# Decoder step on one core: last four experts' token rows normed apart, results written by indirect stores

## The reference

```python
def hier_moe(x, w_rg, b_rg, w_re, b_re, w_e1, w_e3, w_e2):
    ...
    for g in range(N_GROUPS):
        a = jnp.einsum('nd,edf->nef', xf, w_e1[g])
        b = jnp.einsum('nd,edf->nef', xf, w_e3[g])
        hid = jax.nn.silu(a) * b * gates[:, g, :, None]
        y = y + jnp.einsum('nef,efd->nd', hid, w_e2[g])
...
    x = x + hier_moe(rmsnorm(x, g_ffn), w_rg, b_rg, w_re, b_re, w_e1, w_e3, w_e2)
...
    y_prompt = rmsnorm(xp, g_final)
    y_sample = rmsnorm(xs, g_final)
```

## Time and profile before

| what | us |
|---|---|
| median of 3 runs (lowest, highest) | 1066.56 (1065.76, 1069.48) |
| the profiled execution's own time | 1065.81 |
| its span | 1064.0 |
| PE, DVE, ACT, POOL busy | 999.0, 638.3, 541.6, 197.6 |

### The profile page before, as it was taken

The page is one execution under the profiler, slowest core; times in us unless marked ns, Lnnn a source line. Parts: engine busy times, 40 slices in busy tenths (PEclk is TensorE's granted clock), DMA queues, the critical chain, the costliest instruction groups (busy, mean ns, idle before and its releaser), DMA issues. The chain is left out here.

```text
span 1064.0 us, 14237 instructions
## 1 busy us (share of the span) xinstructions
PE 999.0 (94%) x5327; PEld 848.1 (80%) x5327; DVE 638.3 (60%) x1175; ACT 541.6 (51%) x918; POOL 197.6 (19%) x136
## 2 busy tenths in 40 slices
PE   8999999999999999999999999948999999999970
PEld 6998999798887689999655878847888888888850
DVE  4526756345654650002664125677999999999935
ACT  6644333305221532213545012255999999999944
POOL 0003211100000021200000300011333375642220
PEclk9999999999999999999999999967999999999995
DMA  9701111244000653103563005487999999999738
GB/s 314 217 1 59 57 42 40 99 139 173 1 1 0 225 177 113 40 20 127 232 256 139 1 37 201 159 310 300 396 392 391 384 364 390 382 387 393 284 55 335
DMA packets 55211, 203.06 MB, mean 191 GB/s; under 512 B 10710, under 2 KB 19423, under 8 KB 41575
## 3 DMA queue, kind: packets, MB, share of 16 engines
q1 hardware_dynamic: 44327, 181.61, 44.9%
q0 software_dynamic: 10816, 20.54, 7.6%
HBM read 185.06 MB, written 32.83 MB: 205 GB/s over the span
## 5 line engine op out<-in xcount | busy, mean ns | idle before, releaser
L527 PE MATMUL bank<-regA_r,regW_r 128*128 128x352 f32 (+1 forms) x456 | 148.8, 326 | 0.0
L526 PE MATMUL bank<-regA_r,regW_r 128*128 128x352 f32 (+1 forms) x456 | 148.7, 326 | 0.0
L359 POOL TENSOR_TENSOR regW_r<-regW,regW_r 128x1024 fp32r<-128x1024 f32 x19 | 47.1, 2477 | 348.7 <-ACT regW_r L346 348.6
L1525 ACT ACTIVATE regY_r<-expert_w 128x1024 fp32r<-128x1024 f32 x105 | 108.9, 1062 | 1.0 <-PE bank L527 0.9
L525 PE MATMUL bank<-expert_w_r,regS_r 128*128 128x512 f32 x256 | 103.4, 404 | 0.0
L1525 ACT ACTIVATE regW_r<-expert_w 128x1024 fp32r<-128x1024 f32 x87 | 90.2, 1061 | 6.7 <-PE bank L527 6.7
L2292 DVE TENSOR_TENSOR expert_w_r<-expert_w,regY_r 128x1024 fp32r<-128x1024 f32 x74 | 89.0, 1218 | 0.0
L525 PE MATMUL bank<-regY_r,regW_r 128*128 128x352 f32 (+1 forms) x264 | 87.3, 331 | 0.5 <-ACT regB L1206 0.5
L526 PEld LDWEIGHTS bank<-regA_r,regW_r 128*128 128x128 f32 x456 | 85.9, 188 | 0.4
L527 PEld LDWEIGHTS bank<-regA_r,regW_r 128*128 128x128 f32 x456 | 85.6, 188 | 0.0
L2466 POOL DMA_INDIRECT regW<-normed_tokens,idx x32 | 44.0, 1374 | 200.0 <-DVE idx L2201 119.6
(11 more groups left out here) (363 smaller groups left out, 2408.1 us busy)
## 6 DMA issues: line engine op xcount, KB each, us to landing
expert_w<-in_we SPq DMA_DIRECT2D x96, 1024.0 KB, 13.3
regY<-in_cache_mem_v SPq DMA_DIRECT2D x6, 1024.0 KB, 7.2
regW<-in_wbc SPq DMA_DIRECT2D x11, 512.0 KB, 3.6
regS<-in_x_prompt SPq DMA_DIRECT2D x8, 512.0 KB, 6.5
regX<-in_x_prompt SPq DMA_DIRECT2D x8, 512.0 KB, 6.6
regW<-in_wq SPq DMA_DIRECT2D x8, 512.0 KB, 3.6
regA<-in_kct SPq DMA_DIRECT2D x4, 1024.0 KB, 7.9
token_sums<-regX SPq DMA_DIRECT2D x8, 512.0 KB, 2.9
```

The costliest lines, as they stand in the source:

```text
L359: eng.tensor_tensor(lo, raw, hi.bitcast(F32), ALU.subtract).then_inc(w_lo[name], 1)
L526: nc.tensor.matmul(out, stays[1], moves[0], start=False, stop=False)
L527: ins = nc.tensor.matmul(out, stays[0], moves[0], start=False, stop=last)
L1525: nc.scalar.activation(part_hi[u % HI], part_raw[n % RAW], ACT.Copy).then_inc(m_wh, 1)
```

## The change

`LATE = 4` experts (28 to 31 in the order of the loop) no longer add their rows to `token_sums`.

- When the accumulating DMA of expert 27 has landed, SP loads all nine tiles of `token_sums` (the sample tile first) into freed parts of the weight ring (`XF`), and POOL gathers the rows of the last four experts' tokens from it (`late_sums`, into `XR`). The rows hold all that the experts 0 to 27 gave.
- The tiles are squared, normed, scaled and stored as before (`square`, `roots`, `inverse`, `scaled`, `final_store`), but while the last experts run. The sample tile and the first two prompt tiles are scaled in the turn of expert 30 on DVE, and their reciprocal roots are worked out by POOL in 14 small steps (`first_roots`); tile 2 is scaled in turn 31; the others after it.
- The rows of a late expert are added to `XR` on chip: for experts 28 to 30 by POOL (`rows_added`), for expert 31 by DVE straight from PSUM (`last_rows`). ACT squares them, DVE scales them into `YR`, and POOL writes them over the results by plain indirect DMAs (`results_out`): one to `y_sample` and one to `y_prompt` for each late expert, eight in all, those to the prompt only after all prompt tiles' stores have landed. An index out of range for the output writes nothing. Since a token's two experts lie in one group and the four late ones in four groups, no token is in two of them.
- The tail of waits on `o_go` and `s_moe` is gone where there is no spill; with a spill, all is added up and normed once more.

```diff
+        gfin = spot(0)
+        XF = [spot(1 + t) for t in range(NT)]
+        XR = [spot(1 + NT + k) for k in range(LATE)]
+        YR = [spot(1 + NT + LATE + k) for k in range(LATE)]
+        UNITS = [("tile", t) for t in (NPT, *range(NPT))] + [("rows", k) for k in range(LATE)]
+        ROOTS = [(0, 3), (3, 2), (5, 2), (7, 2), (NT, LATE - 1), (NT + LATE - 1, 1)]
...
 # SP
+            for n in range(NT):
+                weights_landed(sp, n)
+            spot_dead(sp, 0)
             load(gfin, i_["gfin"], s_cst)
+            for q in range(2):
+                sp.wait_ge(m_sc[q], 16 * len(range(q, NE - LATE, 2)))
...
+            for _, t in UNITS[:NT]:
+                sums_load(t)
+            for u, (_, t) in enumerate(UNITS[:NT]):
+                sp.wait_ge(s_fo, u + 1)
+                final_store(t)
...
 # ACT
+                if e == NE - 2:
+                    square(0)
+                    square(1)
+                if e == NE - 1:
+                    nc.scalar.activation(small[:, 2:3], small[:, 0:1], ACT.Sqrt)
                 if e >= 1:
                     y_left(e - 1)
...
                 hidden_left(e)
+                if e == NE - 2:
+                    square(2)
+                    square(3)
...
-            y_left(NE - 1)
-            act.wait_ge(o_go, 1)
+            for u, n in ROOTS[1:]:
+                for v in range(max(u, 4), u + n):
+                    square(v)
+                roots(u, n)
...
 # DVE
+                if e == NE - 1:
+                    scaled(2)
                 hidden_lo(e)
+                if e == NE - 2:
+                    dve.wait_ge(s_cst, 32)
+                    dve.wait_ge(s_rt[1], NT + 1)
+                    scaled(0)
+                    scaled(1)
...
+            for k, (u, n) in enumerate(ROOTS[1:]):
+                if k == 1:
+                    last_rows()
+                dve.wait_ge(s_frt, k + 1)
+                inverse(u, n)
+                for v in range(u, u + n):
+                    scaled(v)
...
 # POOL
+            def late_sums():
+
+                for q in range(2):
+                    g.wait_ge(m_sc[q], 16 * len(range(q, NE - LATE, 2)))
+                    g.wait_ge(m_g[q], 16 * (NE // 2))
+                for k in range(LATE):
+                    if k >= 2:
+                        rows_back(g, k - 2)
+                    spot_dead(g, 1 + NT + k)
+                    c = expert_at(NE - LATE + k)
+                    g.indirect_dma_start(out=XR[k], out_offset=None, in_=sum_dram,
...
+            def rows_added(k):
+
+                e = NE - LATE + k
+                rows_back(g, k)
+                g.wait_ge(m_yo0, e + 1)
+                g.wait_ge(m_yo1, e + 1)
+                nc.gpsimd.tensor_tensor(XR[k], XR[k], YO[e % 2], ALU.add).then_inc(s_added, 1)
...
+                if e == NE - LATE:
+                    late_sums()
+                if e > NE - LATE:
+                    rows_added(e - 1 - (NE - LATE))
+                if e == NE - 2:
+                    first_roots()
...
+            g.wait_ge(s_xh_ys, 32)
+            for k in range(LATE - 1):
+                samples_out(k)
+            g.wait_ge(s_fst, 16 * NPT)
+            for k in range(LATE):
+                prompt_out(k)
+            samples_out(LATE - 1)
```

More of the change, by code:

```diff
@@ L59 @@
 LG = 40
+LATE = 4
 NEG = -3.0e38
@@ L455, in trunk_step @@
         o_sc = sem("o_sc")
[L456 removed]
+        s_added = sem("s_added")
+        s_rows = sem("s_rows")
         s_fo = sem("s_fo")
@@ L1190, in _ @@
                                  .rearrange("a p k -> (a p) k")).then_inc(o_ix, 16)
[L1192 to L1200 removed]
+                sp.wait_ge(o_go, 2)
+                for t in range(NT):
+                    sums_load(t)
+                for t in range(NT):
+                    sp.wait_ge(s_fo, NT + t + 1)
+                    final_store(t)
+                sp.wait_ge(s_fst, 16 * 2 * NPT)
+                sp.wait_ge(s_xh_ys, 48)
         @block.scalar
@@ L1249, in _ @@
             nc.scalar.activation(small[:, 1:2], small[:, 0:1], ACT.Sqrt)
-            for h, landed in ((0, s_xh), (1, s_x[0])):
+            for h, landed in ((0, s_xh_ys), (1, s_x[0])):
                 act.wait_ge(landed, 16)
@@ L1572, in _, with square, roots @@
                     part_to_hi("down", 0, 1)
+            def square(u):
+                kind, n = UNITS[u]
+                r = rows_of(n) if kind == "tile" else P
+                if kind == "tile":
+                    sums_back(act, n)
+                elif n < LATE - 1:
+                    act.wait_ge(s_added, n + 1)
+                else:
+                    act.wait_ge(m_yo0, NE)
+                    act.wait_ge(m_yo1, NE)
+                if u > 0:
+                    act.wait_ge(s_fsq, u)
+                nc.scalar.activation(junk[0:r, :], (XF if kind == "tile" else XR)[n][0:r, :], ACT.Square,
+                                     accum_out=stat[0:r, u:u + 1]).then_inc(s_fsq, 1)
+            def roots(u, n):
+                act.wait_ge(s_fsq, u + n)
+                nc.scalar.activation(stat[:, 20 + u:20 + u + n], stat[:, u:u + n], ACT.Sqrt,
+                                     scale=1.0 / D, bias=small[:, 0:1]).then_inc(s_frt, 1)
             for e in range(NE):
@@ L2335, in _, with late_samples, inverse, scaled @@
             down_lo(0, 1)
+            def late_samples():
+                listed_at, samples_at = idx[:, expert_at(NE - LATE):NE:EPG], idx[:, NE:NE + LATE]
+                link(ts_(samples_at, listed_at, float(SEQ), float(NOWHERE), ALU.is_lt, ALU.mult))
+                link(stt(samples_at, samples_at, -float(SEQ), listed_at, ALU.add, ALU.add))
+            def inverse(u, n, r=P):
+                a, root, r0, tmp, out = (stat[0:r, c + u:c + u + n] for c in (40, 20, 60, 80, 100))
+                link(ts_(a, stat[0:r, u:u + n], 1.0 / D, EPS, ALU.mult, ALU.add))
+                inv_root(a, root, r0, tmp, out)
+            def scaled(u):
+                kind, n = UNITS[u]
+                g = stat[:, 100 + u:101 + u]
+                if kind == "tile":
+                    x = XF[n][0:rows_of(n), :]
+                    stt(x, x, g[0:rows_of(n), :], gfin[0:rows_of(n), :], ALU.mult, ALU.mult).then_inc(s_fo, 1)
+                else:
+                    spot_dead(dve, 1 + NT + LATE + n)
+                    stt(YR[n], XR[n], g, gfin, ALU.mult, ALU.mult).then_inc(s_rows, 1)
+            def last_rows():
+                rows_back(dve, LATE - 1)
+                gates = gate_of_slot[:, expert_at(NE - 1):expert_at(NE - 1) + 1]
+                for h, signal in ((0, m_yo0), (1, m_yo1)):
+                    if h == 0:
+                        dve.wait_ge(full[B_Y[0]], uses[B_Y[0]] + 1)
+                    else:
+                        used(dve, ("down", NE - 1, 1))
+                    rows = XR[LATE - 1][:, 512 * h:512 * h + 512]
+                    stt(rows, bank[B_Y[h]][:, :], gates, rows, ALU.mult, ALU.add).then_inc(signal, 1)
             for e in range(NE):
@@ L2352, in _ @@
                     place_in_table((e - 5) // 3)
+                if e == 14:
+                    late_samples()
                 if e == 16:
```

151 lines of the change are left out of this document (98 added, 53 removed).

## The result

| | before | changed |
|---|---|---|
| median of four runs, us | 1066.7 (1065.8 to 1069.5) | 1083.1 (1080.8 to 1083.8) |
| the profiled execution's time and span | 1065.8, 1064.0 | 1080.8, 1078.7 |

The ratio is 1.0141 (95% interval 1.0116 to 1.0165); the medians differ by 16.4 us, the two profiled executions by 15.0. The forecast was 1068.7 (no change), with a range from 1061 to 1075.5; it missed.

A forecast was written before the change was run, and what follows sets the result against it. PE was taken to bound the body, leaving a 32.3 us tail; 10.9 us saved there is given back by a late PE (10.1) and POOL's queue (some 11): span +2.9, time 1068.7 us, range 1061 to 1075.5.

The forecast's parts named there:

- step 4: POOL's eight indirect stores at the end: from 1052.05 to 1064.05, then landing and end, span 1066.9.
- 0.35 for the end: Estimated time from the last store's landing to the end of the span: 0.35 us.
- Step 1, roots at 1029.4: POOL's gathers, two additions and 14 steps of 0.23 us: roots ready at 1029.4, bounds 1026.6 to 1031.1.
- the signs named for being wrong: Second POOL addition ending outside 1024 to 1029, step off 0.23, yy(31) before 1033, equal stores, chain ending on SP.
- Step 2, DVE held, PE late at the low clock: DVE waits for roots, PE idles 8 us, twelve last matmuls take 5.5 us at low clock, to 1041.8.
- Step 3: DVE's roots, last_rows and scalings after the last expert: group (3,2) from 1037.2, expert 31's rows at 1055.85.
- Rival 2: POOL's stores at the end: each plain indirect store takes 1.95 us, 5.7 more, 1074.4; chance 0.25.
- Rival 3: POOL's first small operation in first_roots is slow, at 6 us giving 1074.7; chance 0.05.
- Rival 4: The change does not do what it says: with a spill the norm runs twice; chance next to nothing.
- Rival 1: POOL's roots come early, 4.8 us earlier: 1063.9, or 1062.0 with every store at 1.0 us; chance 0.22.
- The sum: Span 1066.9 against 1064.0, +2.9 us; 1068.7 against the profiled execution's 1065.81: no change.
- Theory E: From the experiments: the 1.85 us ahead of expert 27's DMA are chance, another execution shifting between 0 and 4 us.

The follow-up runs named there:

- e1: Kernel before plus one wait at the end of POOL's program for SP's last nine stores, no work added: 1076.1 us, ratio 1.0074.
- e6: The change with a semaphore for each gather, so the third and fourth don't wait for the first two: 1074.0 us, ratio 1.0058.
- e3: The change without the hold of DVE: all roots on ACT and DVE, all scalings after expert 31's hidden_lo: 1077.3 us, ratio 1.0078.
- e5: e3 with the three additions of late experts' rows on DVE instead of POOL: 1074.2 us, ratio 1.0052.
- e10: e5 with e6's semaphores for the gathers: 1070.6 us, ratio 1.0023.
- e13: e10 with the first root on ACT early in turn 31 and DVE's first scaling before hidden_lo(31): 1069.4 us, ratio 1.0008.
- e17: e13 with stores over four semaphores, four root groups instead of six, first late row tile scaled before the last two tiles: 1067.0 us, ratio 0.9975.
- e8: The changed kernel run again as it is: 1082.7 us, ratio 1.0138.
- e2: The change without its eight indirect stores: 1072.4 us, ratio 1.0040.
- e7: e5 with two late experts instead of four and all squares behind the loop: 1072.6 us, ratio 1.0031.
- e11: e7 with its two gathers on borrowed semaphores: 1074.3 us, ratio 1.0054.
- e4: The change with POOL's third addition waiting until DVE has scaled the first two tiles: 1081.0 us, ratio 1.0117.
- e15: The change with early waits and only the fourth gather on another semaphore, gathers still in series: 1076.6 us, one run.

## Why the prediction was wrong

**The step that failed** is in step 4: "0.35 for the end". From the end of the last store to the end of the span it had 2.85 us (landing 2.5 and this); measured are 9.9, of which 7.9 are POOL's DRAIN. The estimate took the end of a program that ended on SP, whose DRAIN is 7 ns, for one that ends on POOL. 7.0 of the miss are this term alone, and e1 shows it by itself. The row was in the trace of before, at 1039.2, 17 us clear of the end; I had not asked what ends on POOL's queue. With its 7.5 us in place of the 0.35 the forecast would have been some 1075.9, outside the stated range, and none of the rivals had it.

Point by point, with the 1.85 us ahead of expert 27 added to each forecast moment:

- *Step 1, roots at 1029.4*, so 1031.3: they came at 1033.55. Mechanism right. The first gather was issued 0.4 later than said and landed at about 1021 instead of 1020.1; the fourteen steps took 0.27 each, not 0.23 (3.8 us for 3.2), inside the bounds. Two of the signs named for being wrong had come, a step off 0.23 and the second addition ending after 1029 (at 1029.67). The fourth gather, released by the landing of the second, started 1.8 later than said (1023.93 for 1022.15).
- *Step 2, DVE held, PE late at the low clock*: right. `hid` of expert 31 ended at 1040.7 for a forecast of 1036.5: 2.3 from the roots and 2.0 from the clash in `scaled(0)`, which no term had. I had quoted the shared interface for the stores, where the rows leave it at most 1.0 us (below), and not for `rows_added`, an operation with both inputs in SBUF. PE idled 12.3 us, not 8. Seven of the eleven gaps between the starts of the twelve matmuls were 0.43 us, the lower level, and the last two 0.24, the full one: 4.75 us in all for my 5.5, and the last ended at 1047.1.
- *Step 3*: right in its order and its durations; the chain of DVE from its (3,2) group to its end took 18.3 us, and I had 1037.2 to 1055.85, 18.65. It was 3.9 late for the reasons above.
- *Step 4*: eight stores took 10.97 us, 1.0 under my 12.0. The five last, beside nothing, took 0.97 each; the first and the third, beside a scaling on DVE, 1.30 and 1.68, the second, beside DVE's small operations, 0.99. Rival 2, to which I gave 0.25, is out: no plain store took 1.95.
- *Rival 3*, a slow first small operation: out, 0.19 us like the others. *Rival 4*: out. *Rival 1*, roots early: its condition did not come (the first gather was issued at 1014.04, not earlier than forecast). e6 is nearest to its world (first scaling 3.6 us earlier), and it was still 6.3 us over the kernel before, of which 4.85 are the DRAIN.
- *The sum*: 2.9 forecast in the stretch; 2.9 more by steps 1 to 4 and 7.0 by the end give 12.8, measured 12.9. From there to the medians: of the 14.4 us between forecast and median, 10.0 are these two, 1.85 lie ahead of expert 27, 2.3 is what the median lies above the profiled execution, and 0.3 lies outside the span.

By the runs, from the 74.4 us of the change down to 61.5: the hold of DVE and the clash that it hid cost 7.2 of the 74.4 together (e3, e5), the two gathers' semaphores 3.0 by way of the DRAIN (e10), the late first root 2.1 (e13), groups and order 0.6 (e17). Each is a difference of single profiled executions; e8 and e17 show that such a one can be 1.2 to 1.85 us long by chance, so the small ones are rough. What is left in e17 is the 4.85 us of DRAIN and the eight stores; that they eat just what loading the sums under the last experts saves is argued from the equal stretches, no run took them away.

## What to carry to other kernels

Before moving the last work of a kernel to another engine, look at what that engine's queue does after its last instruction: POOL's DRAIN took 4.8 to 7.9 us in all nineteen profiles, and is free only while another engine ends later by that much. Work put on POOL "because it is idle" is not free for DVE: these additions stopped DVE's operations with two inputs in SBUF for nearly as long as they overlapped them (6.4 us of 6.9); on DVE itself the same additions took half the time (1.22 us for 2.36) and PE was not late for them. And when a wait is removed, ask what it was hiding: here the hold covered a clash worth 6.4 us.

## What the runs showed that was not expected

- **POOL's DRAIN** is 7502 ns in the kernel before and in e1, and 7915 in both executions of the change, but differs between programs: 7.50 us (before, e1), 7.59 without stores (e2), 7.79 with four (e7, e11), 7.92 with eight, and 4.85 or 5.51 when the fourth gather signals another semaphore. What it does is open. Among the changed programs more indirect stores go with a longer one, but e2 issues as many indirect DMAs as the kernel before (82) and its DRAIN is 0.09 longer, and the semaphores' effect fits no count that I could form. The DRAIN of PE or DVE can be microseconds too, but covers work that is still open: DVE's in e17 took 5.70 us and ended 0.1 behind its last scaling. POOL's begins when the landings have been waited for.
- **DVE stands still beside a POOL addition**: 6.4 us lost in 6.9 of overlap (e3), 2.0 in 2.2 (the change), 2.15 for an addition of 2.34 (e4).
- **The gathers of the token rows** took 7.1 us from issue to landing beside SP's nine loads (median of the change's profile), near the 6.4 of the one taken from the earlier trace rows; but a second execution of the same program had the first 1.2 us later.
- **The part ahead of expert 27** varied between builds: its DMA came at 1002.49 and 1003.31 with the code of before, and between 1002.16 (e15) and 1006.68 (e2) with that of the change, at 1004.3 in both executions of the changed kernel. From the first scatter on (748.5 in before) all kept the same spacing. One place is seen: after a short idle of PE at 90 to 92 us the changed kernel ran at the lower clock until 97, the kernel before did not, on the same instructions; the same POOL addition then starts at 113.70 instead of 112.00, nearly all of the 1.85. Fourteen of the nineteen profiles have the lower clock between 94 and 96 us, all with code of the change. The five without are the two with the code of before and three of the change's: e3, e13 and e15. e15 was earlier than before, but e13, without that stretch, still came at 1005.02, so there are other places. So the code of the change does not force it; whether it makes it likelier, and what decides, stays open. Theory E is neither shown nor refuted: it repeats for one program, and changes from one to the next.

```profile
90.00:92.00 2.00, 0.72 (x7) 0.32 (x5) 1.38 (x4) 1.98 (x3) 0.00 (x0) 1.00 0.50 137
94.00:96.00 2.00, 2.00 (x8) 2.00 (x7) 1.88 (x5) 1.97 (x8) 0.00 (x0) 0.50 0.03 10
96.00:98.00 2.00, 2.00 (x10) 2.00 (x9) 1.93 (x4) 2.00 (x5) 0.99 (x1) 0.69 0.00 0
```

(The changed kernel, the same table by stretches; the kernel before has 1.00 in all three.)
